# Gate and up projections of two chunk pairs per feed-forward stage with seven block products in place of eight

## What is computed

```python
def _swiglu(h, w_in, w_out):
    gu = h @ w_in                      # (256, 1024) @ (1024, 5632)
    gate, up = jnp.split(gu, 2, axis=-1)
    return (jax.nn.silu(gate) * up) @ w_out    # (256, 2816) @ (2816, 1024)

x = x + 0.5 * _swiglu(_rmsnorm(x, ffn1_norm[l]), ffn1_w_in[l], ffn1_w_out[l])
...
x = x + 0.5 * _swiglu(_rmsnorm(x, ffn2_norm[l]), ffn2_w_in[l], ffn2_w_out[l])
```

## Time and profile before

| | |
|---|---|
| median of 3 runs | 893.57 us (893.34 to 893.6) |
| span of the profiled execution | 892.0 us |
| PE busy | 886.7 us (99%) |
| PE weight loads busy | 730.0 us |
| DVE busy | 564.2 us (63%) |
| ACT busy | 448.7 us (50%) |
| POOL busy | 65.8 us (7%) |
| DMA | 192.75 MB, 216 GB/s mean |

### The profile page before, as it was taken

One profiled execution on the slowest core, in us unless ns is written; L12 is line 12 of the kernel. 1 busy time (PEld: TensorE's weight loads), 2 busy tenths in 40 slices (PEclk: granted clock), 3 DMA queues, 4 the chain that ended last, 5 costly groups with the idle time before them and its releaser, 6 DMA issues.

```text
span 892.0 us, 12022 instructions
## 1 busy us (share of the span) xinstructions
PE 886.7 (99%) x4214; PEld 730.0 (82%) x4214; DVE 564.2 (63%) x761; ACT 448.7 (50%) x522; POOL 65.8 (7%) x115
## 2 busy tenths in 40 slices
PE   9999999999999999999999999999999999999998
PEld 7888888888788888888888888888877888888887
DVE  5765565477977665654575656555689766564562
ACT  6554444457846544544354534444677654444440
POOL 3300000032101000000020000000210110000000
PEclk9999999999999999999999999999999999999999
DMA  9878787783187767777656768786432876776841
GB/s 301 264 252 231 214 257 224 228 236 132 70 272 248 232 219 253 241 238 241 211 183 213 255 201 258 237 269 204 140 133 92 272 241 220 242 252 220 263 141 47
DMA packets 154327, 192.75 MB, mean 216 GB/s; under 512 B 9668, under 2 KB 127240, under 8 KB 154288
## 3 DMA queue, kind: packets, MB, share of 16 engines
q1 hardware_dynamic: 152816, 189.17, 65.9%
q0 software_dynamic: 1296, 2.92, 1.5%
q10 hardware_dynamic: 176, 0.14, 0.0%
HBM read 178.04 MB, written 14.16 MB: 215 GB/s over the span
## 4 chain that ended last, share of the span: by engine, by line
PE 91%; DVE 5%; DMA 2%; issue 1%; ACT 0%; SPq 0%; DVEq 0%; ACTq 0%
PE U L1251 10%; PE U L1254 10%; PE U L1252 10%; PE TR L1251 8%; PE TR L1254 8%; PE TR L1252 8%; PE C L1251 6%; PE C L1254 6%; PE C L1252 6%; PE D L1254 5%; PE D L1252 5%; PE D L1251 5%; DMA h_rows<-qs 2%; DVE sc L1101 1%; DVE w_lo L864 1%; PE U L1296 1%
## 5 line engine op out<-in xcount | busy, mean ns | idle before, releaser
L864 DVE TENSOR_TENSOR w_lo<-raw,w_hi 128x2048 fp32r<-128x2048 f32 x150 | 341.2, 2288 | 109.4 <-ACT w_hi L604 108.9
L604 ACT ACTIVATE w_hi<-raw 128x2048 fp32r<-128x2048 f32 x150 | 284.8, 1910 | 62.9 <-DMA raw<-in_ffn_w_in_dram 49.0
L1251 PE MATMUL U<-w_hi,xT 128*128 128x512 f32 (+1 forms) x448 | 172.6, 385 | 0.0
L1254 PE MATMUL U<-w_hi,xT 128*128 128x512 f32 (+1 forms) x448 | 171.1, 382 | 0.0
L1252 PE MATMUL U<-w_lo,xT 128*128 128x512 f32 (+1 forms) x448 | 171.1, 382 | 0.0
L1251 PE MATMUL TR<-w_hi,xT 128*128 128x512 f32 x320 | 124.7, 390 | 0.0
L1254 PE MATMUL TR<-w_hi,xT 128*128 128x512 f32 x320 | 124.5, 389 | 0.0
L1252 PE MATMUL TR<-w_lo,xT 128*128 128x512 f32 x320 | 124.5, 389 | 0.0
L636 ACT ACTIVATE hT_hi<-gv 128x256 fp32r<-128x256 f32 x78 | 28.4, 411 | 181.4 <-DMA gv<-h_rows 181.4
L1251 PEld LDWEIGHTS U<-w_hi,xT 128*128 128x128 f32 x448 | 84.2, 188 | 16.6
L1254 PEld LDWEIGHTS U<-w_hi,xT 128*128 128x128 f32 x448 | 84.2, 188 | 16.4
(11 more groups left out here) (172 smaller groups left out, 946.6 us busy)
## 6 DMA issues: line engine op xcount, KB each, us to landing
raw<-in_ffn_w_in_dram SPq DMA_DIRECT2D x168, 512.0 KB, 5.7
raw<-in_ffn_w_out_dram SPq DMA_DIRECT2D x88, 512.0 KB, 4.4
raw<-in_w_mix_in_dram SPq DMA_DIRECT2D x28, 512.0 KB, 4.8
h_rows<-qs SPq DMA_DIRECT2D x39, 256.0 KB, 4.8
gv<-h_rows SPq DMA_DIRECT2D x156, 64.0 KB, 2.0
raw<-in_w_mix_out_dram SPq DMA_DIRECT2D x16, 512.0 KB, 4.0
raw<-in_ffn_w_in_dram SPq DMA_DIRECT2D x16, 256.0 KB, 4.4
bias<-bias_rows POOLq DMA_DIRECT2D x8, 192.0 KB, 6.9
```

The lines of the kernel that those rows point to most:

```text
L604: act.activation(w_hi[:, p % SLOTS, :], raw[:, p % RAW, :], ACT.Copy).then_inc(hi_ready, 1)
L864: dve.tensor_tensor(w_lo[:, p % SLOTS, :], raw[:, p % RAW, :], w_hi[:, p % SLOTS, :].bitcast(F32), ALU.subtract).then_inc(lo_ready, 1)
L1251: pe.matmul(out_, x_hi, w_hi[:, slot, c], start=start, stop=False, skip_group_check=reopened)
L1254: last = pe.matmul(out_, x_lo, w_hi[:, slot, c], start=False, stop=stop, skip_group_check=reopened)
```

## The change

Two pairs of chunks per stage, (3, 4) and (7, 8), get a new scheme (the code calls a pair a quad, by its first chunk, 3 or 7). Let X be cut into four blocks by token tile (0, 1) and contraction half, and the pair's weights into four blocks: contraction half (first digit) by gate (1) or up (2), each with the 512 columns of both chunks. These are the units B11, B12, B21, B22, 1 MiB each. DVE adds whole units to make four more right-hand operands T1 to T4 (`add_term`, in place in the raw buffers), and combines the input blocks into four new left-hand operands `x5, x7, x6, x3` (`combine_x`), once per stage. Seven products of one dozen each (`term_product`) replace the eight of the two chunks' `enter`. Three partial sums are copied out of PSUM in between (`copy_sum`, ACT) and added to others (`add_gate`, `add_up`, DVE). For each pair two trips through DRAM (one per token tile, for both chunks: `store_h`/`store_g`) replace two trips (one per chunk).

To make room, `w_hi`/`w_lo` have 5 slots, `raw` has 5 buffers, `bias` shares memory with the input combinations and is loaded once per layer. All loops in the stages are unrolled; raw buffers are assigned by a small planner (`places`), the one that is free first by the order in which the lo parts are made.

```diff
-SLOTS = 6
-RAW = 3
+SLOTS = 5
+RAW = 5
...
+QUADS = (3, 7)
+    def quad(c):
+        term = {n: (s, "sum", c, n) for n in TERMS}
+        return [term["B11"], term["B21"], term["T1"], term["T2"], (s, "out", c - 1), term["T3"], term["T4"], term["B22"],
+                *inner(c + 2), (s, "out", c), (s, "out", c + 1), *inner(c + 3), (s, "out", c + 2)]
```

PE, a pair (`term_product` is 12 matmuls, `leave` waits for the trip as before):

```diff
+                def quad(c):
+                    a, b, d = [x_[:, :] for x_ in QUAD_BANKS[c]]
+                    pe.wait_ge(h_done, H_ORDER[s, c - 2, 1])
+                    term_product(s, c, "B11", a)
+                    term_product(s, c, "B21", b)
+                    pe.wait_ge(h_done, H_ORDER[s, c - 1, 0])
+                    pe.wait_ge(xc_lo_done, 4 * (s + 1))
+                    term_product(s, c, "T1", d)
+                    pe.wait_ge(sums_copied, SNAP_ORDER[s, c, "s1"])
+                    term_product(s, c, "T2", a)
+                    leave(c - 1, 0)
+                    pe.wait_ge(sums_copied, SNAP_ORDER[s, c, "s2"])
+                    term_product(s, c, "T3", a)
+                    leave(c - 1, 1)
+                    pe.wait_ge(sums_copied, SNAP_ORDER[s, c, "s3"])
+                    term_product(s, c, "T4", a)
+                    pe.wait_ge(sums_added, SUM_ORDER[s, c, "up1"])
+                    term_product(s, c, "B22", d)
...
+                    for t in (1, 0):
+                        leave(c, t)
+                        leave(c + 1, t)
```

For a pair, first DVE's list, then ACT's (`term` is the split of a unit):

```diff
+                def pair(c):
+                    if c == 3:
+                        combine_x(s)
+                    term(c, "B11")
+                    rest_h(s, c - 2)
+                    if c == 3:
+                        rest_x(s)
+                    term(c, "B21")
+                    multiply(s, c - 1, 0)
+                    multiply(s, c - 1, 1)
+                    turn_h(s, c - 1)
+                    add_term(s, c, "T1")
+                    add_term(s, c, "T3")
+                    term(c, "T1")
+                    add_term(s, c, "T2")
+                    term(c, "T2")
+                    out(c - 1)
+                    add_gate(s, c)
+                    rest_h(s, c - 1)
+                    term(c, "T3")
+                    add_term(s, c, "T4")
+                    term(c, "T4")
+                    term(c, "B22")
+                    add_up(s, c, 1)
+                    made(c + 2, 0)
+                    made(c + 2, 1)
+                    multiply_pair(s, c, 1)
+                    turn_h(s, c)
+                    add_up(s, c, 0)
+                    multiply_pair(s, c, 0)
+                    turn_g(s, c)
...
+                def pair(c):
+                    term(c, "B11")
+                    round_h(s, c - 2)
+                    if c == 3:
+                        x_hi(s)
+                    term(c, "B21")
+                    silu(s, c - 1, 0)
+                    silu(s, c - 1, 1)
+                    term(c, "T1")
+                    copy_sum(s, c, "s1")
+                    term(c, "T2")
+                    out(c - 1)
+                    round_h(s, c - 1)
+                    term(c, "T3")
+                    copy_sum(s, c, "s2")
+                    silu_pair(s, c, 0)
+                    term(c, "T4")
+                    term(c, "B22")
+                    copy_sum(s, c, "s3")
...
```

SP, at the entrance and for a pair:

```diff
+                load_out(s, 1)
+                load_block(s, 3, "B11")
+                load_block(s, 3, "B12")
+                if by_trip(s, 0):
+                    store_h(s, 0)
+                    load_block(s, 3, "B21")
+                    load_h(s, 0)
...
+                store_h(s, 1)
+                load_block(s, 3, "B22")
+                load_h(s, 1)
+                load_out(s, 2)
...
+                    inner(c + 3)
+                    if c == 3:
+                        store_h(s, 5)
+                        load_h(s, 5)
+                        load_out(s, 5)
+                        for name in ("B11", "B12", "B21", "B22"):
+                            load_block(s, 7, name)
```

More of the change, by code:

```diff
@@ new lines, in stage_used, with later, whole @@
+def stage_used(s):
+    made = stage_made(s)
+    def later(a, b):
+        made.remove(a)
+        made.insert(made.index(b) + 1, a)
+    if s > 0:
+        later((s, "out", 0), (s, "in", 2, 0))
+    for c in QUADS:
+        later((s, "out", c - 1), (s, "sum", c, "T3"))
+    return made
+def whole(stage):
+    out = []
+    for L in range(LAYERS):
+        out += stage(2 * L) + [(2 * L, "mix", n) for n in MIX] + stage(2 * L + 1)
+    return out
+MADE, USED = whole(stage_made), whole(stage_used)
@@ new lines, with loads_of, freed_by, places @@
+NTH_MADE = {u: i for i, u in enumerate(MADE)}
+NTH_USED = {u: i for i, u in enumerate(USED)}
+def loads_of(u):
+    if u[1] != "sum":
+        return [u]
+    return [(u[0], "sum", u[2], n) for n in ("B11", "B12", "B21", "B22")] if u[3] == "B11" else []
+LAST_READ = {"B11": "T4", "B12": "T3", "B21": "T4", "B22": "B22"}
+def freed_by(load):
+    return load if load[1] != "sum" else (load[0], "sum", load[2], LAST_READ[load[3]])
+def places():
+    slot, before, count = {}, {}, {}
+    holds = [None] * RAW
+    turns = [0] * RAW
+    for load in [x for u in MADE for x in loads_of(u)]:
+        r = min(range(RAW), key=lambda i: (-1 if holds[i] is None else NTH_MADE[freed_by(holds[i])], i))
+        before[load], slot[load] = holds[r], r
+        holds[r] = load
+        turns[r] += 1
+        count[load] = turns[r]
+    return slot, before, count
@@ new lines, with raw_of, slot_of, n_made @@
+RAW_SLOT, RAW_BEFORE, RAW_COUNT = places()
+RAW_OF = {"B11": "B11", "B21": "B21", "B22": "B22", "T1": "B11", "T2": "B11", "T4": "B11", "T3": "B12"}
+HT_SLOT = {0: 0, 1: 1, 2: 0, 3: 0, 4: 1, 5: 0, 6: 1, 7: 0, 8: 1, 9: 1, 10: 0}
+def raw_of(u):
+    return RAW_SLOT[u if u[1] != "sum" else (u[0], "sum", u[2], RAW_OF[u[3]])]
+def slot_of(u):
+    return NTH_MADE[u] % SLOTS
+def n_made(u):
+    return NTH_MADE[u] + 1
+def n_used(u):
+    return NTH_USED[u] + 1
+def counts(of_stage):
+    return {(s, *e): i + 1 for i, (s, e) in enumerate((s, e) for s in range(2 * LAYERS) for e in of_stage(s))}
@@ new lines, in split_rest, with add_term @@
+                lo_of(u, slice(UNIT // 2, UNIT)).then_inc(lo_ready, 1)
+            def add_term(s, c, name):
+                to, other = {"T1": ("B11", "B12"), "T2": ("B11", "B22"), "T3": ("B12", "B22"), "T4": ("B11", "B21")}[name]
+                r, n = landed((s, "sum", c, other))
+                dve.wait_ge(unit_loaded[r], n)
+                if name == "T3":
+                    r, n = landed((s, "sum", c, to))
+                    dve.wait_ge(unit_loaded[r], n)
+                a, b = [raw[:, RAW_SLOT[s, "sum", c, x_], :] for x_ in (to, other)]
+                dve.tensor_tensor(a, a, b, ALU.add).then_inc(terms_added, 1)
@@ L891, in multiply, with add_gate, add_up @@
                 last.then_inc(h_done, 1)
-            def turn_h(L, f, c, j=0):
-                dve.wait_ge(h_done, n_ffn(L, f, c, 1, j))
+            def add_gate(s, c):
+                dve.wait_ge(sums_copied, SNAP_ORDER[s, c, "s1"])
+                dve.wait_ge(units_used, n_used((s, "sum", c, "B21")))
+                dve.tensor_tensor(s1, s1, QUAD_BANKS[c][1][:, :], ALU.add).then_inc(sums_added, 1)
+            def add_up(s, c, t):
+                to, name, after = (s2, "s2", "B22") if t == 0 else (s3, "s3", "T3")
+                dve.wait_ge(sums_copied, SNAP_ORDER[s, c, name])
+                dve.wait_ge(units_used, n_used((s, "sum", c, after)))
+                dve.tensor_tensor(to, to, QUAD_BANKS[c][2][:, :], ALU.add).then_inc(sums_added, 1)
@@ L1036, in ffn @@
+                multiply(s, 1, 0)
+                multiply(s, 1, 1)
+                if by_trip(s, 0):
+                    rest_h(s, 0)
+                turn_h(s, 1)
+                made(2, 1)
+                out(1)
+                for c in QUADS:
+                    pair(c)
                 if f == 0:
                     layer_gains(L)
-                split(L, pos_out(f, 10))
-                rest_h(L, f, 9)
-                multiply(L, f, 10, 0)
+                out(10)
+                rest_h(s, 9)
@@ L1041, in ffn @@
+                multiply(s, 10, 0)
                 if after is not None:
-                    split(L, after[0])
+                    split(after[0])
                 elif L < DEPTH - 1:
```

860 lines of the change are left out of this document (500 added, 360 removed).

## The result

The changed kernel takes 982.91 us (981.62 to 987.06), against 893.59 us for the kernel before on the same chip: a ratio of 1.1005, 95% interval 1.0982 to 1.1029. It is slower by 89 us. The forecast, 928.4, has the direction; the time lies above its range.

A forecast was written before the change was run, and what follows sets the result against it. PE, busy 99%, was taken as the bound. Removing matmuls saves 21.8 us, but waits on DVE's list and late loads leave a net +34.8 us: 893.6 + 34.8 = 928.4 us, range 885 to 975 (its own 905 to 955).

The forecast's parts named there:

- The sum: Whole kernel: pair costs 3 x 6.7 + 2.3 + 4 x 3.1 = +34.8 us, put on the median of 893.6.
- What is removed: PE, eight pairs: seven dozens of matmuls for eight, 2.72 us a pair, -21.8 us if PE never waits.
- The prices: DVE and ACT work: whole-unit adds 2.21 us each on DVE, splits 2.29 or 2.21, small ones 0.66.
- The chain in a pair: DVE's list after the turn: T1's lo at t+6.6, T2's at t+12.9, both inputs of T4 at t+25.3.
- The t that it starts from: End of chunk c-1's turn on DVE, from PE's due start of B11: -0.5 in quad 7, +0.7 in later stages' quad 3.
- t + 6.3: How late PE starts T4 in a pair; against the 2.72 us saved, a pair costs t + 3.6.
- The waits forecast for hT_lo and before T4: PE in each pair: about 0.9 us for hT_lo and 0.6 us before T4.
- rival 4: PE's clock falls after waits for T1 and T2: 5.4 us x 8 more, 972 us; chance 0.15.
- Rival 3: The pair's DRAM trips meet weights, 9.9 instead of 5.4 us: 36 us more, 964 us; chance 0.13.
- The entrances: Starts of three stages: PE waits 2.4 us each for chunk 0, whose trip stands behind weight loads.
- The best a pair can do is nothing gained: Each pair: the earliest turn, at -3.65 us, only cancels the saving; any lateness of t adds in full.
- The range: Total time: 905 to 955 us from t's spread, 885 to 975 with most of the rivals.

The follow-up runs named there:

- e_both: Changed kernel with SP's, ACT's and DVE's lists reordered in several steps, lastly a residual ahead of a mixing-weight split: 893.4 us, ratio 0.9990 against the kernel before.
- a_rounds_first: Changed kernel with ACT and DVE taking chunk 5's round and rest ahead of out 5 and B11 in the pair of chunk 7: 981.9 us.
- a_busy_pe: Changed kernel plus unused matmuls on PE, 8 before the product of T1 and 9 before that of T2: 975.7 us.
- a_end_store: Changed kernel with SP storing chunk 9 before the loads of out 9, and loading it before out 10 and the next part's first unit: 980.3 us.
- b_early_adds: Changed kernel with only DVE's adds moved: T1's ahead of the turn, T3's behind T2's, T4's ahead of out and the chunk's rest: 954.3 us.

## Why the prediction was wrong

Two steps failed. The sum took the clock at 0, with no more reason than that no row priced a wait, and it cost 24.2 us. And it ended with the pairs, so that the trip of chunk 9 at a stage's end wasn't in it at all: 17.7 us.

1. **What is removed** was right: 96 matmuls, 21.8 us. In e_both PE's busy time is below that of before.
2. **The prices** were right for whole units. Adds took 2.29 for one and 4.45 for two in a row (mean 2.275; forecast 2.21). The small ones were taken at 0.66, said to be 0.69 less the overlap of the splits, but 2.29 - 2.21 = 0.08 gives 0.61, and the rows above start 0.60 apart; over a stage's eight this is 0.5 us. DVE's busy time was 715.7 for 731.
3. **The chain in a pair** was right as to mechanism and length: 6.6 and 13.0 us from the turn to the two lo parts, for 6.6 and 12.9. The t that it starts from was put too early on the whole. In the pair of chunk 3 of the second stage the turn ended at 339.63 and PE wanted T1 at 343.45, so t = 339.63 - (343.45 - 5.44) = +1.6, forecast +0.7; in the pair of chunk 7, 411.17 - (415.99 - 5.44) = +0.6, forecast -0.5. Over all eight pairs t ran from -2.0 to +2.1. By the forecast's t + 6.3 the eight should have waited 49 us. They waited 41.6, and half-speed matmuls in them cost another 16.7: 58. The waits forecast for hT_lo and before T4 didn't come where PE was slow in between; in a_rounds_first, where four of the waits for T2 were followed by full speed, hT_lo was waited for again, 0.54 to 0.56 us.
4. **The clock, taken at 0, failed** as a size: this was rival 4, put at up to 43 us with a chance of 0.15, and it measured 24.2. a_busy_pe shows that the waits cause it. The Trainium skill's sentence (TensorE: Matmul & The Clock Gate, Part 1) that idleness takes full clock back holds here, though not behind each wait: 3.65 us at 134.99 are followed by 13 half-speed matmuls, 2.91 us at 518.59 by none.
5. **A path was absent.** What the new order of SP does at `leave(5)` and at the stage's end was never asked. Those are 7.7 and 17.7 us. Rival 3 had the mechanism, a trip that meets weights, but for the pair's own trips, where it brought one wait of 1.5 us. The kernel before had no slack at the stage's end. There PE waited for the same product once, at 177.14, and SP's rows of the trip were these:

```profile
PE TR L1378 <- DVE small L882: 0.3, 1, 0.3
```
```profile
165.04 0.34 SPq L423 DMA_DIRECT2D h_rows<-qs  x1
172.28 1.75 SPq L430 DMA_DIRECT2D gv<-h_rows  x4
```

   The store of chunk 9 stands behind the same weights of `out` and of the next part in SP's list before and after. But the two units of chunk 10, asked for from 141.43 on before, now stand behind the pair's two stores, and these wait for DVE's turns. SP's wait between 148 and 175 us in the changed kernel:

```profile
SPq L538 <- DVE qs L1165: 7.0, 1, 7.0
```

   From 166.46 on SP finds every buffer free and asks for 5 MiB in 6.5 us, and the store gets in behind them. So it is the order of SP's list that bunches the weights, and not a lack of buffers. a_end_store moves the store ahead, and its load goes out 13 us sooner (177.96); the bunch itself wasn't taken away alone. The 7.7 us proved to cost nothing (a_rounds_first), which the chain of step 3 explains: T1's lateness counts from DVE, not from PE's arrival. That same rule shows that a sum of waits is not a sum of costs.
6. **The entrances**: 9.9 us. Of it 7.1 at chunk 0 of three stages, for 7.2 forecast; the waits for chunk 1 and for the input weren't forecast.
7. **"The best a pair can do is nothing gained"** holds for the order as built, and isn't a bound of the scheme. It took the order of DVE's list as given: 25.3 us from turn to T4, with T1's add behind the turn and T3's ahead of T1's split. b_early_adds moved adds alone for -28.6. In e_both the pairs wait 0.5 us before T4 and under 1 before T2.
8. **The range.** Its terms reach from 904 to 946, not to 955, and each rival was added to the forecast alone. What came was the forecast, the clock and a missing path together.

So the miss of 54.5 us is: clock 24.2, stage ends 17.7, pairs a net -7.6, entrances and other waits 7.2, `leave(5)` 7.7, uneven spacing 3.5. That is 52.7. (The pairs' -7.6 and the 7.7 of `leave(5)` belong together: without the latter T1 waits longer.) What bounded the changed kernel was the order of three lists, and the adds cost what they did because of it: e_both has the same 857 instructions on DVE and is 89.5 us faster. That the scheme couldn't pay even then was shown only for the orders tried. A still better one isn't excluded; a raw buffer more, which might let T2's add run ahead of T1's split, wasn't tried.

## What to carry to other kernels

Price a new chain from the moment that starts it, and then ask, for every list that the change touches, what each later item now stands behind when transfers bunch up: here the stage ends waited 17.7 us for that, most of the 21.8 that the arithmetic saved. Look for the paths that have no slack already: before the change PE waited 0.3 us in one of these places. A saving on the busiest engine is worth its time only while that engine never waits, and waits cost more than themselves: 24.2 us of half speed for 81.4 us of waits. And when the work still fits on average (53 of 62.6 us), move one item of the list at a time, follow the wait to its next place, and expect gains of single moves to add up to less than their sum.
